# Second gated FFN's up projection: pairs of panels from the third on as seven block products

## The reference, cut to what matters

```
D_MODEL = 1024; SEQ = 512; D_FF = 2816

def swiglu(x, w_gate, w_up, w_down):
    return (jax.nn.silu(x @ w_gate) * (x @ w_up)) @ w_down

    h = h + 0.5 * rms_norm(swiglu(rms_norm(h, ffn2_pre_g[i]), ffn2_w_gate[i], ffn2_w_up[i], ffn2_w_down[i]),
                           ffn2_post_g[i])
```

## Time and profile before

| | us |
|---|---|
| median of three runs | 3027.21 |
| lowest and highest | 3024.95, 3027.63 |
| span of the profiled execution, first to last instruction | 3022.4 |
| mean granted TensorE clock | 0.987 of full |

### The profile page before, as it was taken

The page is one execution under the profiler, slowest core; times in us unless marked ns, Lnnn a source line. Parts: engine busy times, 40 slices in busy tenths (PEclk is TensorE's granted clock), DMA queues, the critical chain, the costliest instruction groups (busy, mean ns, idle before and its releaser), DMA issues.

```text
span 3022.4 us, 36545 instructions
## 1 busy us (share of the span) xinstructions
PE 2902.0 (96%) x12794; PEld 2213.6 (73%) x12802; DVE 1803.7 (60%) x2790; ACT 903.8 (30%) x1606; POOL 294.4 (10%) x213
## 2 busy tenths in 40 slices
...
GB/s 150 109 109 122 104 75 79 63 70 56 49 78 70 90 97 94 96 68 87 86 77 66 77 90 97 97 93 82 87 42 36 36 29 91 82 92 97 97 93 96
DMA packets 78549, 249.86 MB, mean 83 GB/s; under 512 B 8840, under 2 KB 15368, under 8 KB 78440
## 3 DMA queue, kind: packets, MB, share of 16 engines
...
...
## 4 chain that ended last, share of the span: by engine, by line
PE 87%; DVE 7%; ACT 3%; issue 2%; DMA 0%; ACTq 0%; POOL 0%; SPq 0%; DVEq 0%; POOLq 0%
PE ps L317 24%; PE ps L318 24%; PE ps L319 24%; PE ps L3385 1%; PE ps L3430 1%; PE ps L3406 1%; PE ps L3407 1%; PE ps L906 1%; PE ps L2902 1%; DVE w_lo L300 1%; PE ps L2178 1%; DVE w_hi L291 1%; PE ps L2887 1%; PE ps L2157 1%; PE ps L1545 1%
## 5 line engine op out<-in xcount | busy, mean ns | idle before, releaser
L317 PE MATMUL ps<-xh,w_hi 128*128 128x512 f32 x2152 | 881.2, 409 | 40.6 <-DVE xl L487 13.3
L318 PE MATMUL ps<-xl,w_hi 128*128 128x512 f32 x2152 | 855.7, 398 | 0.0
L319 PE MATMUL ps<-xh,w_lo 128*128 128x512 f32 x2152 | 855.3, 397 | 0.0
L291 DVE CAST w_hi<-raw 128x1024 fp32r<-128x1024 f32 (+1 forms) x438 | 302.5, 691 | 736.2 <-PE ps L319 700.5
L317 PEld LDWEIGHTS ps<-xh,w_hi 128*128 128x128 f32 x2152 | 407.1, 189 | 185.4 <-issue 54.0
L300 DVE TENSOR_TENSOR w_lo<-raw,w_hi 128x1024 fp32r<-128x1024 f32 (+1 forms) x386 | 502.5, 1302 | 28.5
L319 PEld LDWEIGHTS ps<-xh,w_lo 128*128 128x128 f32 x2152 | 406.8, 189 | 100.0
L318 PEld LDWEIGHTS ps<-xl,w_hi 128*128 128x128 f32 x2152 | 407.9, 190 | 98.4 <-issue 7.2
L317 PE MATMUL ps<-ah,w_hi 128*128 128x512 f32 x704 | 278.1, 395 | 0.0
L318 PE MATMUL ps<-al,w_hi 128*128 128x512 f32 x704 | 278.1, 395 | 0.0
L319 PE MATMUL ps<-ah,w_lo 128*128 128x512 f32 x704 | 278.1, 395 | 0.0
...
## 6 DMA issues: line engine op xcount, KB each, us to landing
raw<-in_ffn_up SPq DMA_DIRECT2D x90, 512.0 KB, 3.3
raw<-in_conv_up SPq DMA_DIRECT2D x88, 512.0 KB, 3.2
raw<-in_ffn_down SPq DMA_DIRECT2D x32, 512.0 KB, 3.6
raw<-in_conv_down SPq DMA_DIRECT2D x32, 512.0 KB, 3.5
raw<-in_merge SPq DMA_DIRECT2D x24, 512.0 KB, 3.2
raw<-in_ple_gate SPq DMA_DIRECT2D x24, 512.0 KB, 3.2
raw<-in_diff SPq DMA_DIRECT2D x24, 512.0 KB, 3.3
raw<-in_mla SPq DMA_DIRECT2D x20, 512.0 KB, 3.2
```

What stands on the lines that cost most here:

```text
L291: dve.tensor_copy(self.w_hi[s][:, 0:n], self.raw[r][:, 0:n]).then_inc(self.sem["slot_hi"], 1)
L317: pe.matmul(out, wh, xh, start=start, stop=False)
L318: pe.matmul(out, wh, xl, start=False, stop=False)
L319: return pe.matmul(out, wl, xh, start=False, stop=stop)
```

## The change

A new class `SevenUp` takes the place of `SwigluUp` in the second FFN. Its first round (two pairs, panels 0 to 3) is as before. Each of the 20 pairs from the third on is taken as a 2 x 2 matrix of blocks, gate and up panel by the two halves of the contraction (128 x 512 each, four blocks of 128 x 128), times a 2 x 2 matrix of the tokens' features (two halves of the contraction by two halves of 256 tokens). The four result blocks come from seven block products P1 to P7 instead of eight, each 4 x 3 = 12 matmuls of 256 columns:

- The left factors: P1 and P2 take the gate panel's halves, P4 the up panel's second half, and P5, P6, P7 and P3 the sums S1 to S4 of halves (S1 on POOL, in place; S2 to S4 on DVE, into PSUM banks 0 and 1).
- The right factors: for P1, P2 and P3 parts of `xh` and `xl`; for the others four mixtures of token blocks, made once at the start of the stage (`tf`, with high and low parts `th` and `tl`).
- Each left factor gets a high part on ACT (`block_high`) and a low part on DVE (`sum_low`: P5, P6, P7, P3) or POOL (`panel_low`: P1, P2, P4), in a ring of four half slots.
- P1, P6, P7 and P4 add up in one PSUM region, P5 and P3 in another, P2 in a third. ACT copies out P1, P5 and P1+P6 on the way, and DVE adds the quarters C11, C22 and C12 and scales C21; then it scales the pair by `rs`, which ACT has put into PSUM bank 3.
- PE's order for pair n: P1(n), P7(n-1), P3(n-1), P5(n), P4(n-1), P6(n), P2(n); after the last pair P7, P3 and P4 of it.
- The loads of the stage from pair 2 on wait for S4 and two low parts of the pair two before. At the end `take_over` on DVE raises the counts of the shared slots at once, so that the next stage's loads can go on.

```diff
--- before.py
+++ after.py
...
+        self.th = sb("th", [P, 4, 4, T // 2], F32R)
...
+            [("_hole11", [P, 28 * T], F32), ("xf", [P, KD, T], F32), ("tf", [P, 4, 4, T // 2], F32),
+             ("tl", [P, 4, 4, T // 2], R)],
...
+class SevenUp(SwigluUp):
...
+    PAIRS = KF - 2
+    RING, AHEAD, HALF = 4, 3, T // 2
+    STEP = {"P1": 0, "P7": 1, "P3": 2, "P5": 3, "P4": 4, "P6": 5, "P2": 6}
+    SUM = {"P5": "S1", "P6": "S2", "P7": "S3", "P3": "S4"}
+    OUT = {"P1": "X", "P6": "X", "P7": "X", "P4": "X", "P2": "Y", "P5": "Z", "P3": "Z"}
...
+    def low_made(self, n, which):
+        return self.of("sum_lo" if which in self.SUM else "panel_lo", (n, which))
...
+    def left(self, n, which):
+        return {"P1": self.gate_raw(n, 0), "P2": self.gate_raw(n, 1), "P5": self.up_raw(n, 0), "P6": self.k.ps[:, 0, :],
+                "P7": self.k.ps[:, 1, :], "P3": self.k.ps[:, 0, :], "P4": self.up_raw(n, 1)}[which]
...
+    def sync(self, sp):
+        k = self.k
+        for q in range(8):
+            k.load(sp, self.w, q // 4, q % 4, self.weights[q])
+        for n in range(2, self.PAIRS):
+            for up, last in ((0, "P2"), (1, "P4")):
+                i, pos = self.place(n, up)
+                sp.wait_ge(*self.of("sum_made", (n - 2, "S4")))
+                sp.wait_ge(*self.low_made(n - 2, last))
+                sp.dma_start(k.raw[pos][:], self.weights[4 * i + pos]).then_inc(k.landed[pos], 16)
...
+    def seven(self, pe, n, which):
+        k, s, half, out = self.k, self.index[n, which], self.HALF, self.sums_of(n)[self.OUT[which]]
+        pe.wait_ge(*self.low_made(n, which))
+        if which == "P1" and n >= 2:
+            pe.wait_ge(*self.of("c_made", (n - 2, "C21")))
+        if which == "P5":
+            pe.wait_ge(*(self.of("c_made", (n - 2, "C12")) if n >= 2 else self.on("rstd")))
+        if which == "P2":
+            pe.wait_ge(*(self.of("c_made", (n - 1, "C11")) if n else
+                         (k.sem["gate_scaled"], self.e.at("gate_scaled", 1))))
+        if which == "P6":
+            pe.wait_ge(*self.of("copied", (n, "P1")))
+        if which == "P3":
+            pe.wait_ge(*self.of("copied", (n, "P5")))
+        if which == "P7":
+            pe.wait_ge(*self.of("copied", (n, "P1+P6")))
+        if which == "P4":
+            pe.wait_ge(*self.of("c_made", (n, "C22")))
+        wh, wl = self.ring(k.w_hi, s), self.ring(k.w_lo, s)
+        for t in range(4):
+            if which in ("P1", "P2", "P3"):
+                x, own = t + 4 * (which != "P1"), slice(half * (which == "P3"), half * (which == "P3") + half)
+                xh, xl = k.xh[:, x, own], k.xl[:, x, own]
+            else:
+                c = {"P5": 0, "P6": 1, "P7": 2, "P4": 3}[which]
+                xh, xl = k.th[:, t, c, :], k.tl[:, t, c, :]
+                if n == 0 and which in ("P5", "P7"):
+                    pe.wait_ge(*self.of("t_lo", (t, c // 2)))
+            col = slice(t * P, (t + 1) * P)
+            pe.matmul(out, wh[:, col], xh, start=which in ("P1", "P2", "P5") and t == 0, stop=False, skip_group_check=True)
+            pe.matmul(out, wh[:, col], xl, start=False, stop=False, skip_group_check=True)
+            mm = pe.matmul(out, wl[:, col], xh, start=False, stop=t == 3, skip_group_check=True)
+        mm.then_inc(k.sem["block_used"], 1)
...
+    def tensor(self, pe):
+        if self.own:
+            self.source.mean(pe)
+        self.first_round(pe)
+        for n in range(self.PAIRS):
+            self.seven(pe, n, "P1")
+            if n:
+                self.seven(pe, n - 1, "P7")
+                self.seven(pe, n - 1, "P3")
+            self.seven(pe, n, "P5")
+            if n:
+                self.seven(pe, n - 1, "P4")
+            self.seven(pe, n, "P6")
+            self.seven(pe, n, "P2")
+        self.seven(pe, self.PAIRS - 1, "P7")
+        self.seven(pe, self.PAIRS - 1, "P3")
+        self.seven(pe, self.PAIRS - 1, "P4")
...
+    def fourth_high(self, act):
+        k = self.k
+        i, pos = 0, 3
+        act.wait_ge(k.landed[pos], self.w.landed(i, pos))
+        act.wait_ge(k.sem["slot_used"], self.w.split_free(i, pos))
+        act.activation(k.w_hi[pos % 2][:], k.raw[pos][:], ACT.Copy).then_inc(k.sem["slot_hi"], 1)
...
+    def block_high(self, act, s):
+        k = self.k
+        if s >= len(self.blocks):
+            return
+        n, which = self.blocks[s]
+        if s >= self.RING:
+            act.wait_ge(*self.of("block_used", s - self.RING))
+        else:
+            act.wait_ge(k.sem["slot_used"], self.w.used(0, 2 + s // 2))
+        if which == "P5":
+            act.wait_ge(*self.of("sum_first", n))
+        elif which in self.SUM:
+            act.wait_ge(*self.of("sum_made", (n, self.SUM[which])))
+        else:
+            i, pos = self.place(n, which == "P4")
+            act.wait_ge(k.landed[pos], self.w.landed(i, pos))
+        act.activation(self.ring(k.w_hi, s), self.left(n, which), ACT.Copy).then_inc(k.sem["block_hi"], 1)
...
+    def keep_rs(self, act):
+        k = self.k
+        act.wait_ge(k.sem["up_scaled"], self.e.at("up_scaled", 1))
+        act.wait_ge(*self.on("rstd"))
+        act.activation(k.ps[:, 3, :], k.rs[:], ACT.Copy).then_inc(k.sem["rs_kept"], 1)
...
+    def copy(self, act, n, of, c):
+        k, which = self.k, {"P1": "P1", "P5": "P5", "P1+P6": "P6"}[of]
+        act.wait_ge(*self.used(n, which))
+        if n < 2:
+            act.wait_ge(k.sem["act_lo"], self.e.at("act_lo", n))
+        else:
+            act.wait_ge(*self.of("product" if of == "P5" else "silu", n - 2))
+        act.activation(self.quarter(n, c), self.sums_of(n)[self.OUT[which]], ACT.Copy).then_inc(k.sem["copied"], 1)
...
+    def scalar(self, act):
...
+        self.block_high(act, 0)
+        self.block_high(act, 1)
+        self.first_high(act, 0)
+        self.first_silu(act, 1)
+        self.block_high(act, 2)
+        self.mixed_high(act, 0, 1)
+        self.mixed_high(act, 1, 1)
+        for n in range(self.PAIRS):
+            self.block_high(act, self.index[n, "P1"] + self.AHEAD)
+            if n == 0:
+                self.first_high(act, 1)
+                self.mixed_high(act, 2, 1)
+                self.mixed_high(act, 3, 1)
+                self.keep_rs(act)
+            if n >= 2:
+                self.pair_high(act, n - 2)
+            self.copy(act, n, "P1", "C11")
+            if n:
+                self.block_high(act, self.index[n - 1, "P7"] + self.AHEAD)
+                self.block_high(act, self.index[n - 1, "P3"] + self.AHEAD)
+            self.block_high(act, self.index[n, "P5"] + self.AHEAD)
+            self.copy(act, n, "P5", "C22")
+            if n:
+                self.pair_silu(act, n - 1)
+                self.block_high(act, self.index[n - 1, "P4"] + self.AHEAD)
+            self.block_high(act, self.index[n, "P6"] + self.AHEAD)
+            self.copy(act, n, "P1+P6", "C12")
+            self.block_high(act, self.index[n, "P2"] + self.AHEAD)
+        self.pair_high(act, self.PAIRS - 2)
+        self.pair_silu(act, self.PAIRS - 1)
+        self.pair_high(act, self.PAIRS - 1)
...
+    def sum_low(self, dve, n, which):
+        k, s = self.k, self.index[n, which]
+        dve.wait_ge(*self.of("block_hi", s))
+        dve.tensor_tensor(self.ring(k.w_lo, s), self.left(n, which), self.ring(k.w_hi, s).bitcast(F32), ALU.subtract
+                          ).then_inc(k.sem["sum_lo"], 1)
...
+    def s2(self, dve, n):
+        k = self.k
+        i, pos = self.place(n, 0)
+        dve.wait_ge(*self.of("sum_first", n))
+        dve.wait_ge(k.landed[pos], self.w.landed(i, pos))
+        if n:
+            dve.wait_ge(*self.low_made(n - 1, "P3"))
+        dve.tensor_tensor(k.ps[:, 0, :], self.up_raw(n, 0), self.gate_raw(n, 0), ALU.subtract).then_inc(k.sem["sum_made"], 1)
...
+    def c11(self, dve, n):
+        own = self.quarter(n, "C11")
+        dve.wait_ge(*self.of("copied", (n, "P1")))
+        dve.wait_ge(*self.used(n, "P2"))
+        dve.tensor_tensor(own, self.sums_of(n)["Y"], own, ALU.add).then_inc(self.k.sem["c_made"], 1)
...
+    def c22(self, dve, n):
+        own = self.quarter(n, "C22")
+        dve.wait_ge(*self.of("copied", (n, "P5")))
+        dve.wait_ge(*self.used(n, "P7"))
+        dve.tensor_tensor(own, self.sums_of(n)["X"], own, ALU.add).then_inc(self.k.sem["c_made"], 1)
...
+    def pair_product(self, dve, n):
+        k, b = self.k, n % 2
+        dve.wait_ge(*self.of("up_scaled", n))
+        dve.wait_ge(*self.of("silu", n))
+        dve.tensor_tensor(k.sq[b][:], k.tmp[2 * b + 1][:], k.sq[b][:], ALU.mult).then_inc(k.sem["product"], 1)
...
+    def vector(self, dve):
...
+        for n in range(1, self.PAIRS):
+            self.c11(dve, n - 1)
+            self.sum_low(dve, n, "P5")
+            self.s2(dve, n)
+            self.c22(dve, n - 1)
+            self.sum_low(dve, n, "P6")
+            self.c12(dve, n - 1)
+            self.pair_gate(dve, n - 1)
+            self.s3(dve, n)
+            self.s4(dve, n)
```

(52 more changed lines are left out.)

211 lines of the change are left out of this document (209 added, 2 removed).

## The result

The changed kernel takes 3033.08 us (median of 10 runs, 3031.35 to 3034.73), the kernel before 3025.22 us in the runs beside it (3023.24 to 3027.63): a ratio of 1.0026, with an interval of 1.0017 to 1.0035. It is slower by 7.9 us; faster by 10.9 us was forecast. The time lies inside the stated range, near its upper end, and on the other side of the kernel before. The span of the profiled execution went from 3022.4 to 3031.0 us.

What follows compares the result with a forecast made beforehand. PE was taken as the bound. Pairs -19.0 and one-time terms +8.1 gave -10.9 us: span 3022.4 to 3011.5, with 4.8 carried over 3016.3 us. Its own range was 3011 to 3022, the stated range 3002 to 3035.

Steps and rivals of the forecast that it cites:

- What bounds the kernel now: Up projection of the second gated FFN: PE time saved is time saved, until DVE, POOL or a load comes last.
- Rivals 2: Matmuls of the 20 changed pairs follow at the weight loads' pace, 0.1125 us: 9.45 a pair, 3000.3 us; chance 0.05.
- 3 (0.1265): Each matmul spacing has 0.020 us fixed: 10.63 a pair, 3023.9 us, no measurable change; chance 0.21.
- 5 (0.187): Weight loads of the changed pairs' matmuls don't hide: 15.7 us a pair, 3125 us; chance 0.03.
- Work added to DVE and POOL: Changed pairs: DVE 8.3 us plus 1.7 lost to POOL, 10.0; with 0.3 of waits on PE's 9.95, 10.25 a pair.
- -19.0: Forecast gain in us over the 20 changed pairs: 205.0 instead of 224.0, at 10.25 a pair.
- the fourth: Three SBUF operations on DVE each lose a whole POOL operation: 11.0 to 12.2 us, middle 11.6, 3043.3 us; chance 0.14.
- Rival 1: PE alone sets the changed pairs' pace, as POOL is held, not DVE: 9.95 a pair, 3010.3 us; chance 0.15.
- The -0.3: Start of the blocks: panel 2's cast no longer waits behind 1/rms, giving back PE's 0.31 us.
- Start: First pair's P6 waits for ACT's copy of P1, queued behind eight operations: +2.7 us (2.4 to 3.4).
- Take-over: Down projection's first load waits for DVE's raise of slot_split after C22 of the last pair: +3.3 us (2.9 to 4).
- Clock: PE at half speed behind the two new gaps, 1.6 us for the longer and half for the shorter: +2.4 (0 to 3.2).

## Why the prediction was wrong

- **What bounds the kernel now**: right. DVE came last, as the paragraph's last sentence allows.
- **One matmul of 256 columns**: right. 0.1185 us was forecast; 0.1183 is measured where PE has no gap (1352 in 160 us), 84 of them 9.95 us, the forecast's number. Rivals 2 (0.1125), 3 (0.1265) and 5 (0.187) fall. The formula in the Trainium skill (TensorE: Matmul & The Clock Gate, Back-to-back issue gap), which the page gives for the gap of a single matmul, makes 109 ns of 256 columns; this format takes more here, 118, as it does at 512 columns (233 against 216).
- **Work added to DVE and POOL: the step that failed.** The price of one meeting was near (0.88 forecast, 1.03 to 1.09 measured: 1716, 1763 and 1778 ns less 0.69). The mistake was the factor of 0.64: POOL's busy share was taken as a chance of meeting, operation by operation. Here the two engines repeat one order every pair and don't meet by chance: from DVE's third turn on they stand in a fixed phase, in which all three operations meet POOL in each pair (1.71 to 1.73, 1.75 to 1.77 and 1.77 to 1.78 us, but for the last product, when POOL has no S1 left). That is 3.2 us instead of 1.7. DVE's chain came to 11.13 us, where 10.0 was forecast and 10.25 for the pair; its bound for the case that each is hit, 10.9, was nearer. So -19.0 became -5.7, or -1.2 at the pace of 11.14 alone.
- **The rival that came true is the fourth**, at its lower end: DVE 11.0 with its operations overlapping by 0.08, against 11.13. It had 0.14. Its reason against, that eleven operations read PSUM, was true (those of 128x512 keep 684 to 696 ns) and had no weight: three are enough. Rival 1 falls too: DVE is held and not POOL alone. What was left out is that the meetings hang together: freeing any one, or moving one by 0.6 us, brings the pair to 9.95.
- **The one-time terms**, +8.1 forecast, came to more. The -0.3 came, as 0.6. Start: 2.7 forecast, 4.4 measured; ACT's queue was read rightly, but DVE's mixtures were taken as ready, and they wait for POOL as well. Take-over: 3.3 forecast, 4.4 measured; the raise was placed behind C22, and it was P4's low part on POOL that came last, 1.6 us later. Clock: 2.4 forecast, 4.7 measured: 0.54 from 978 to 984 us, and 0.50 behind the second gap. The length of the gap alone doesn't settle this term: in the run with the early raise the first gap was 4.22 us as well, and the clock was back at 1.00 from 982 us on. In the changed kernel:

```profile
978.00:984.00 6.00, 5.78 (x29) 0.54 0.15 34
```

```profile
1200.48:1205.40 4.92, 4.92 (x12) 0.50 0.61 189
```

- **Two slips without weight.** POOL's 1.48 us in the earlier trace rows is no loss: L1104 takes 1436 to 1487 ns in all its 44 executions in the kernel before, so DVE alone is held there. And the ends that the prediction gives add up to 3010 to 3024 us, not to 3011 to 3022. Neither changes the forecast.
- The rule on the shared access to SBUF in the Trainium skill (SBUF — State Buffer, Who interferes with whom), by which the engine that issues second waits for the whole instruction of the first, holds here: the product, 0.12 us behind S1, ends 0.55 us after it, and where DVE comes first (P5's low part moved to POOL) it is S1 that takes 1728 ns.

Settled in part: DVE's first two turns in the changed kernel, product to product, take 10.15 and 10.07 us, and each from the third on 11.12 to 11.15. The trace shows the step between. In the first two turns P5's low part keeps 0.68 us, and it is POOL's last operation of the pair (L1333) that is held, 1.84 and 1.62 us; it starts 0.02 us ahead of P5's low part and then 0.20 behind it. In the third turn it starts 0.08 us ahead, and from then on P5's low part waits. The second turn and the third:

```profile
1005.10 1.62 POOL L1333 TENSOR_TENSOR al<-sq,ah 128x512 fp32r<-128x512 f32 x1 [1.60 <-ACT ah L1069]
...
1014.88 1.29 POOL L1333 TENSOR_TENSOR al<-sq,ah 128x512 fp32r<-128x512 f32 x1 [1.33 <-ACT ah L1069]
```

```profile
1004.90 0.68 DVE L1131 TENSOR_TENSOR w_lo<-raw,w_hi 128x512 fp32r<-128x512 f32 x1
...
1014.96 1.76 DVE L1131 TENSOR_TENSOR w_lo<-raw,w_hi 128x512 fp32r<-128x512 f32 x1
```

What brought POOL's operation forward was not tried.
